# Another order of softplus, pool sums, gate sums, key turning and level pieces in the front stage of a hybrid encoder kernel

## What is computed

```python
h = rmsnorm(x, norm_g)
z = einsum('bsd,de->bse', h, w_in)        # 2272 columns, split into:
(c_q, c_kv, k_rope, gate_mla, u_pool, gate_pool,
 q_gla, k_gla, v_gla, lr_fwd, lr_bwd, gate_gla) = split(z)
# pool mixer: centred means of u_pool over windows 2/4/8/16, minus itself, then w_pool and pool_scale
# log gates of the gated linear attention (GLA), one set per direction:
g = log_sigmoid(lr @ gk_up + gk_bias) / 16
# GLA in chunks of 64 tokens, forward and backward:
b = cumsum(g) in the chunk
state = exp(b_last) * state + (k * exp(b_last - b)).T @ v
o     = (q * exp(b)) @ state + sum over j of q_i * exp(b_i - b_j) * k_j * v_j
mixed = [o_mla * silu(gate_mla), o_pool * silu(gate_pool), o_gla * silu(gate_gla)]
out   = rmsnorm(x + mixed @ w_out)
```

## Time and profile before

| what | value |
|---|---|
| median of 3 runs | 882.99 us (880.18 to 885.93) |
| the profiled execution's own time | 884.8 us |
| its span, first to last instruction | 883.0 us |
| mean granted TensorE clock | 0.952 |
| PE busy | 777.1 us, 88% of the span |
| DVE, ACT, POOL busy | 403.6, 335.9, 196.3 us |

### The profile page before, as it was taken

The page is one execution under the profiler, slowest core; times in us unless marked ns, Lnnn a source line. Parts: engine busy times, 40 slices in busy tenths (PEclk is TensorE's granted clock), DMA queues, the critical chain, the costliest instruction groups (busy, mean ns, idle before and its releaser), DMA issues. The chain is left out here.

```text
span 883.0 us, 14305 instructions
## 1 busy us (share of the span) xinstructions
PE 777.1 (88%) x5936; PEld 642.9 (73%) x5936; DVE 403.6 (46%) x699; ACT 335.9 (38%) x572; POOL 196.3 (22%) x223
## 2 busy tenths in 40 slices
PE   3999978579999999999791789999999975999996
PEld 2786856467888788888681578888788873788885
DVE  5635741147444521000184366666666767343332
ACT  6442623324454433211341345444444445222221
POOL 2221312426444421211114000000000007322220
PEclk9999998799999999999885899999999996999999
DMA  7401012000111111130334100000006003254431
GB/s 264 128 19 48 25 59 71 24 2 26 62 62 62 61 50 61 72 131 1 83 127 109 46 16 22 13 13 13 13 13 226 1 1 120 91 172 148 149 125 54
DMA packets 32444, 61.37 MB, mean 69 GB/s; under 512 B 3297, under 2 KB 16001, under 8 KB 32385
## 3 DMA queue, kind: packets, MB, share of 16 engines
q1 hardware_dynamic: 26384, 46.36, 16.4%
q10 hardware_dynamic: 6000, 14.16, 4.1%
HBM read 42.42 MB, written 17.69 MB: 68 GB/s over the span
## 5 line engine op out<-in xcount | busy, mean ns | idle before, releaser
L77 PE MATMUL psum<-h_hi,z_w_hi 128*128 128x512 f32 x432 | 175.5, 406 | 3.8 <-DVE h_lo L697 3.8
L78 PE MATMUL psum<-h_lo,z_w_hi 128*128 128x512 f32 x432 | 169.9, 393 | 0.0
L79 PE MATMUL psum<-h_hi,z_w_lo 128*128 128x512 f32 x432 | 169.7, 393 | 0.0
L77 PEld LDWEIGHTS psum<-h_hi,z_w_hi 128*128 128x128 f32 x432 | 82.4, 191 | 24.8 <-DVE h_lo L697 4.7
L79 PEld LDWEIGHTS psum<-h_hi,z_w_lo 128*128 128x128 f32 x432 | 82.1, 190 | 17.8
L78 PEld LDWEIGHTS psum<-h_lo,z_w_hi 128*128 128x128 f32 x432 | 82.2, 190 | 16.5 <-issue 0.7
L1545 ACT ACTIVATE a_weights<-psum,a_bias,mla_q_scale 128x1024 f32<-128x1024 f32 (+1 forms) x48 | 51.1, 1064 | 104.0 <-DVE a_bias L1584 104.0
L77 PE MATMUL psum<-o_w_hi,o_m_hi 128*128 128x512 f32 x192 | 77.1, 401 | 13.6 <-DVE o_w_lo L1872 13.2
L79 PE MATMUL psum<-o_w_hi,o_m_lo 128*128 128x512 f32 x192 | 76.2, 397 | 0.0
L78 PE MATMUL psum<-o_w_lo,o_m_hi 128*128 128x512 f32 x192 | 76.2, 397 | 0.0
L1608 DVE TENSOR_TENSOR a_turned_lo<-psum,a_turned_hi 128x512 fp32r<-128x512 f32 x80 | 52.3, 687 | 41.7 <-ACT a_turned_hi L1562 41.6
(11 more groups left out here) (209 smaller groups left out, 1493.0 us busy)
## 6 DMA issues: line engine op xcount, KB each, us to landing
z_w_raw<-in_w_z_dram SPq DMA_DIRECT2D x17, 512.0 KB, 3.5
n_x_in<-in_x_dram SPq DMA_DIRECT2D x12, 512.0 KB, 4.1
gates_scratch<-z_gate ACTq DMA_DIRECT2D x24, 256.0 KB, 2.0
o_x_in<-in_x_dram SPq DMA_DIRECT2D x12, 512.0 KB, 3.6
out_dram<-o_y ACTq DMA_DIRECT2D x12, 512.0 KB, 2.6
o_w_raw<-in_w_out_dram SPq DMA_DIRECT2D x8, 512.0 KB, 9.6
a_q_rope<-rope_scratch SPq DMA_DIRECT2D x12, 256.0 KB, 2.6
o_gate_first<-gates_scratch SPq DMA_DIRECT2D x6, 512.0 KB, 4.8
```

What stands on the lines that cost most here:

```text
L77: nc.tensor.matmul(out, a_hi, b_hi, start=first, stop=False)
L78: nc.tensor.matmul(out, a_hi, b_lo, start=False, stop=False)
L79: return nc.tensor.matmul(out, a_lo, b_hi, start=False, stop=last)
```

## The change

All edits lie in the front stage, with no arithmetic added or removed:

- Softplus: both directions' Abs, then both Exp at i = 7, both Ln at i = 8, in place of one direction at 7 and 8 and the other at 9 and 10. A second buffer (`z_soft_second`, in memory where the states come later) makes that possible. It needs 128 bytes of padding behind the states; the second raw weight tile moves inside the same region.
- DVE: the second pool tile's windows ahead of both gate sums. POOL: its layout ahead of `split_lo(4)`.
- PE: pool heads at i = 12, 13, 14 instead of 13, 14, 15. ACT: `take_pool` at the same i ahead of `empty(i)`, where it stood behind it.
- Keys: ACT's `take_keys(0, 1)` and `decay_keys(2, 3)` ahead of `empty(15)` instead of behind it; `turn_keys(2, 3)` in the middle of block 16 instead of the start of 17, and their ACT work at 16; `add_up(0, 1)` at the start of block 18 instead of its middle. POOL: `split_lo(7)` behind `key_exponents(0)` and `weight_decayed(4, 5)` instead of ahead of them.
- ACT: values at 16, 17, 18 instead of 17, 18, 19, and `exponentials(0)` at 17 instead of 19.
- `gla_point` gives one less: each level piece comes half a block later.

```diff
 def gla_point(i, half):
-    return 2 * (i - FIRST_LEVEL_BLOCK) + half
+    return 2 * (i - FIRST_LEVEL_BLOCK) + half - 1
...
+        sb("z_state_pad", [P, P // 4])
...
-        over_state = Region(nc, state_at, state_at + 2 * DV * CHUNKS * 4)
-        w_second = over_state("z_w_raw_second", [P, D_MODEL])
+        over_state = Region(nc, state_at, state_at + 2 * DV * CHUNKS * 4 + P)
         scan_keep = over_state("z_scan_keep", [P, CHUNKS * (CHUNK + 1)])
+        soft_second = over_state("z_soft_second", [P, NT])
...
-            def soften(d):
-                act.wait_ge(biased, TB * (d + 1))
-                if d:
-                    act.wait_ge(log_step, 2)
...
+            def soften():
+                act.wait_ge(biased, 2 * TB)
+                act.wait_ge(w_lo_ready, 2)
+                for d in range(2):
+                    nc.scalar.activation(soft[d][:, :], log_gate[:, d, :], ACT.Abs).then_inc(soft_step, 1)
+                for d in range(2):
+                    act.wait_ge(soft_step, d + 1)
+                    nc.scalar.activation(soft[d][:, :], soft[d][:, :], ACT.Exp, scale=-1.0).then_inc(soft_step, 1)
...
-                if i == 17:
-                    take_values(0)
-                    take_values(1)
+                if i in (12, 13, 14):
+                    take_pool(i - 12)
+                if i == 15:
+                    take_keys(0)
+                    take_keys(1)
+                    decay_keys(2)
+                    decay_keys(3)
+                if i == 16:
                     take_keys(2)
                     take_keys(3)
                     decay_keys(4)
                     decay_keys(5)
-                if i == 18:
+                    take_values(0)
+                    take_values(1)
+                if i == 17:
                     take_values(2)
                     take_values(3)
+                    exponentials(0)
+                if i == 18:
                     take_keys(4)
                     take_keys(5)
-                if i == 19:
                     take_values(4)
                     take_values(5)
-                    exponentials(0)
...
                 if i == 7:
-                    soften(FWD)
+                    soften()
                 if i == 8:
-                    finish_softening(FWD)
-                if i == 9:
-                    soften(BWD)
-                if i == 10:
-                    finish_softening(BWD)
-                if i in (13, 14, 15):
-                    take_pool(i - 13)
+                    finish_softening()
...
             lay_out_pool(0)
+            lay_out_pool(1)
             split_lo(4)
-            lay_out_pool(1)
...
-            split_lo(7)
             key_exponents(0)
             weight_decayed(4)
             weight_decayed(5)
+            split_lo(7)
...
             pool_windows(0)
+            pool_windows(1)
             add_up_gates(FWD)
-            pool_windows(1)
             add_up_gates(BWD)
...
-                    if i in (13, 14, 15):
-                        pool_heads(i - 13)
+                    if i in (12, 13, 14):
+                        pool_heads(i - 12)
...
-                    if i == 17:
-                        turn_keys(2)
-                        turn_keys(3)
                     if i == 18:
                         turn_keys(4)
                         turn_keys(5)
+                        add_up(0)
+                        add_up(1)
...
+                    if i == 16:
+                        turn_keys(2)
+                        turn_keys(3)
```

More of the change, by code:

```diff
@@ L157, in phase_front @@
         eps = sb("n_eps", [P, 1])
-        over_state = Region(nc, state_at, state_at + 2 * DV * CHUNKS * 4)
-        w_second = over_state("z_w_raw_second", [P, D_MODEL])
+        over_state = Region(nc, state_at, state_at + 2 * DV * CHUNKS * 4 + P)
         scan_keep = over_state("z_scan_keep", [P, CHUNKS * (CHUNK + 1)])
+        soft_second = over_state("z_soft_second", [P, NT])
+        w_second = Region(nc, state_at + CHUNKS * (CHUNK + 1) * 4, state_at + 2 * DV * CHUNKS * 4)("z_w_raw_second", [P, D_MODEL])
         over_lr = Region(nc, Z_LR * NT * 4, (Z_LR + 1) * NT * 4)
@@ L174, in phase_front @@
         log_gate = soften_mem("z_log_gate", [P, 2, NT])
-        soft = soften_mem("z_soft", [P, NT])
+        soft = [soften_mem("z_soft", [P, NT]), soft_second]
         pool_mem = Region(nc, Z_Q * NT * 4, (Z_V + 2) * NT * 4)
@@ L385, in store_gate, with finish_softening @@
                   .then_inc(gate_stored[i % 2], 16)
-            def soften(d):
-                act.wait_ge(biased, TB * (d + 1))
-                if d:
-                    act.wait_ge(log_step, 2)
[L391 to L397, removed]
+            def soften():
[6 more added lines that the diff above has]
+                    nc.scalar.activation(soft[d][:, :], soft[d][:, :], ACT.Exp, scale=-1.0).then_inc(soft_step, 1)
+            def finish_softening():
+                for d in range(2):
+                    act.wait_ge(soft_step, d + 3)
+                    nc.scalar.activation(soft[d][:, :], soft[d][:, :], ACT.Ln, bias=1.0).then_inc(soft_step, 1)
             def decays():
@@ L570, in _ @@
                     decay_keys(1)
[L571 to L575, removed]
             act.wait_ge(pool_stored, 16 * TB)
@@ L706, in add_up_gates @@
             def add_up_gates(d):
-                dve.wait_ge(soft_step, 3 * d + 3)
+                dve.wait_ge(soft_step, d + 5)
                 flat = sums[d][:, :, :].rearrange("p c t -> p (c t)")
@@ L711, in add_up_gates @@
                                                in0=log_gate[:, d, :].rearrange("p (c t) -> p c t", t=CHUNK), scalar=0.0,
-                                               in1=soft[:, :].rearrange("p (c t) -> p c t", t=CHUNK),
+                                               in1=soft[d][:, :].rearrange("p (c t) -> p c t", t=CHUNK),
                                                op0=ALU.min, op1=ALU.subtract).then_inc(log_step, 1)
@@ L1076, in mixing @@
                         turn_values(2 * (i - 16) + 1)
-                    if i == 18:
-                        add_up(0)
-                        add_up(1)
                 p = gla_point(i, half)
```

## The result

| | before | changed |
|---|---|---|
| median | 883.19 us (880.18 to 885.93, 4 runs) | 853.0 us (852.05 to 854.39, 4 runs) |
| ratio | 1 | 0.9677, 95% interval 0.9648 to 0.9706 |
| span of the profiled execution | 883.0 us | 852.1 us |
| mean granted clock | 0.952 | 0.966 |

The change makes the kernel 30.2 us faster by the medians and 30.9 by the spans of the two profiled executions. In a second comparison the changed kernel took 853.1 us against 881.8 (0.9671, interval 0.9647 to 0.9696).

A forecast was written before the change was run, and what follows sets the result against it. PE was taken as the bound, with a 24.1 us hole of waits from 106 to 212 us. Idle 21.8 plus clock 7.3 gave 29.1 us off 884.8: 855.7 profiled, about 854 us median, range 848 to 865.

The forecast's parts named there:

- First pool head: PE ahead of block 12: wait for pool windows falls from 3.1 to 0.9 us, saving 2.2 and 1.7 of slow clock.
- The other heads: Two later pool heads on PE: their 4.6 us wait for ACT's `take_pool` goes.
- First keys, the narrowest place: Block 15: keys ready at 126.7, 2 us before PE arrives at 128.7; 2.8 us of slow clock goes.
- Third pair of keys: Keys 4, 5 ready at about 142.5, PE wants them at 148.5; 9.6 us wait and 2.8 of slow clock go.
- Values and states: Values' 1.7 us wait goes; forward scan's wait falls from 3.2 to 2.4 us (bounds 1 to 3.2), saving 0.8.
- Level pieces: Half a block later: first piece's 1.9 us wait goes, 1.0 of the outputs' 1.4 counted, no odd-piece wait taken.
- Table loads: ACT loses two table loads of 1.28 us each while idle there: nothing gained.
- B: Rival, 22%: DVE's windows or gate sums run late, first head and keys wait, 9.6 us given back, 863.5 us.
- C: Rival, 6%: PE's clock falls on sixteen turns in a row and at block 18, twice 2.8 us, 860 us.
- D: Rival, 6%: the time moves, an unseen engine becomes the bound in the level stage; within 1%, 875 to 890 us.
- E: Rival, 3%: slower, odd pieces' `spread_states` late on ACT so six outputs wait; 6.4 us at each gives 892 us.
- clock term: PE's half-level clock behind three waits: 1.7 + 2.8 + 2.8 = 7.3 us saved.

The follow-up runs named there:

- softplus alone: Kernel before with only the softplus edit (second buffer, both directions' Abs, Exp and Ln together): 883.8 us against 883.29, ratio 1.0011.
- keys first: Kernel before with one edit, POOL's `split_lo(7)` behind the level exponents and third pair of decayed keys: 870.4 us, ratio 0.9868.
- copies behind: Changed kernel with ACT's `take_pool` put back behind emptying the block, heads still at blocks 12 to 14: 857.49 us, 0.9728 of the kernel before.
- pool part alone: Kernel before with only the softplus and pool edits (second buffer, earlier pool layout, windows and heads, `take_pool` ahead of `empty`): 871.77 us, ratio 0.9891.

## Why the prediction was right, point by point

- **What bounds the kernel.** Right: PE, and a hole made by waits. The gain arrived in full at the end of the front stage.
- **First pool head.** Forecast a wait between 0 and 1.8, taken as 0.9; measured 1.06. The windows started at 92.8 (forecast 93.4) and ended at 107.2, between 105.6 and 107.7; the collision of 2.1 us happened, at another row than the one seen before. The Trainium skill, "SBUF — State Buffer", in its section "SBUF: two separate sides", says that a DVE instruction with two SBUF inputs and a GpSimd one that reads SBUF contend for one shared pair of ports, and that the one that starts first has it for its whole length. The trace agrees at both meetings. The window row started 0.15 us into the first split and took 2.15 us longer. The second split started while the row ahead of the scan still ran, took 3.57 us for 2.4, and the scan behind it took 2.08 us longer. With that rule the prediction had a wait of 2.0 us, by a start at 93.4 and 2.3 us of collision; both were somewhat too long. The step that a wait of 1.84 us leaves the clock alone was wrong as a rule: the heads took 1.98 us behind a wait of 1.06 in all eight traces that have one, but not behind every wait of 1.84 in the kernels above. That the 1.7 us were saved rests on the wait having come out short.
- **The other heads.** Right, 4.6 us gone; put back, 3.7 us of waits return.
- **First keys, the narrowest place.** No wait. PE asked at 128.88 (forecast 128.7); POOL's last product ended at 127.3 (126.7), so 1.5 us were to spare where the forecast had 2.
- **Third pair of keys.** Right, 9.6 us gone, ready at 143.4 (142.5) for a PE that asks at 148.8 (148.5). Alone it is worth 12.1 us.
- **Values and states.** 1.7 gone as said. The scan's wait was mis-sized, 1.4 for the 2.4 taken and inside the bounds of 1 to 3.2: the two weighted products ahead of it took 1.83 us together, since POOL's own products were over by then (158.2).
- **Level pieces.** The 1.9 and 1.4 us are gone. Of the six odd pieces none waits for ACT where a `compare` stands ahead of the output; the last output, which has none, waits 0.77 us. The 0.6 us that the forecast had for a `compare` of no length is this case.
- **Table loads.** Nothing, shown alone.
- **Sum.** Idle: forecast 21.8; measured 25.5 of waits in the earlier trace rows less 3.3, 22.2 us (the `issue` rows are left out, 1.1 us before and 1.5 now). The front stage ended 31.1 us earlier, and 0.2 us of that stood already at 68 us, ahead of the first changed call (DVE's first gate bias at 68.51 before and 68.26 now). So 8.7 us are left for the clock and what goes with it, where the term was 7.3. That is the term that was too small. Part of it is the wait for the scan, left uncounted: its 192 product rows took 2.92 us before, at a clock of 0.52, and 2.11 now, at 1.00. The rest, about 0.6 us, is not assigned.
- **Rivals.** Of B the premise came true and the consequence did not: DVE lost 4.2 us to the two splits, as B supposed. But only the 2.15 us at the windows stand ahead of the first head, and the 2.08 us at the scan are ahead of the keys, where ACT came to its part at 122.5 us, behind `empty(13)`, and found DVE's decays done at 121.0. So no 4 us wait, and no late keys. For C, sixteen turns in a row ran at full pace (1.04 us for eight, twice) and the small products behind the last keys took 1.51 us, both at a granted clock of 1.00: it did not happen. D and E did not happen; of E one place in six is real, with 0.8 us. Two of the signs that the prediction names for being wrong are there all the same, a window row well above 1.8 us (3.91) and a new wait for spread states (0.8). Each was true and too small to move the result.

The forecast of 854 us is 1 us above the 853.0, or 29.1 us of gain for 30.2. Like with like, the profiled execution was forecast at 855.7 and took 853.9, 1.8 us less. The terms that gave more than counted are the scan's wait (1.0 us) and the clock behind waits (1.4); the first head (0.2) and the outputs (0.4) gave less. The clock term of 7.3 us was read from one execution. The trace of softplus alone has nearly the same waits and loses the time at other heads, yet needs 315.4 us from the first head to the last projection step, for 316.3 before: as a sum the term held, where its single parts are partly luck.

## What to carry to other kernels

In a program of hand-ordered lists, a wait that stays at 9.6 us when PE comes to it 12 us earlier is a chain from PE's own block and back: find the instruction on a third engine that stands ahead of the late one and waits for that block, and put it behind. Price it as idle time plus the slow stretch behind it, and check the next engine's slack at each moved call before adding gains. A helper engine's collisions cost only where someone waits; move them there where nobody does.

## What the runs showed of the hardware

- **A wait's price in clock varies from one execution to the next.** Behind waits of 1.84 us the heads took 1.98 us (before), 3.30 (keys first), 3.23 (softplus alone), 3.15 and 1.98 (the two of one trace with the copies behind); behind 2.79 us 3.78 (before) and twice 1.98 (keys first, softplus alone). The same wait of 9.6 us is followed by 6.55 us (before), 6.16 (softplus alone) and 5.60 (pool part alone) from the third pair of keys to the turned values behind it; a pair without a wait needs 3.62. The prediction took the pattern of one trace as the rule. The runs of the kernel before differ more (878.5 to 886.0 in 17 runs) than those of the changed kernel (851.2 to 854.4 in 9); that would follow from fewer waits, but wasn't tested apart.
- **DVE gets busier without more work.** Its busy time rose from 403.6 to 417.1 us with the same 699 instructions. Of the 13.5 us, 7.8 are at the level exponents of DVE (L761, L763), which now run at the same time as POOL's, and 4.3 at its weighted queries (L772). DVE in the changed kernel:

```profile
130.32 0.28 DVE L763 TENSOR_TENSOR g_q_level<-gate_sums 128x128 f32<-128x128 f32 x1
...
130.93 2.50 DVE L761 TENSOR_TENSOR g_q_level<-gate_sums 128x128 f32<-128x128 f32 x1
...
137.19 0.49 DVE L761 TENSOR_TENSOR g_q_level<-gate_sums 128x128 f32<-128x128 f32 x1
```

The same form takes 0.28 us alone, 2.50 beside the weight split and 0.49 beside POOL's exponents. It cost nothing: DVE had 14.3 us of idle before its next needed row.
